# A two-layer network and a mixture-of-experts block: the two heads of a pair of attention heads taken half a step apart

## What is computed

```python
def mla_attention(q_nope, q_rope, k_nope, k_rope, v):      # 16 heads, 64 + 32 wide, values 64
    def block(args):                                        # one block of 128 queries
        s = (q_nope @ k_nope + q_rope @ k_rope) * scale
        s = where(chunk_mask(qpos, kpos), s, -inf)          # keys up to the query's chunk of 64
        return softmax(s) @ v
h = x + (mla_attention(...) * silu(gate)) @ w_o

def windowed_gqa(q, k, v, rel_bias, sink):                  # 8 heads of 64, 2 heads of keys
    def one_block(i):                                       # 128 queries, the keys of 3 blocks
        logits = where(valid, q @ k * scale + bias, -inf)
        m = maximum(max(logits), sink)
        p = exp(logits - m);  denom = sum(p) + exp(sink - m)
        return (p / denom) @ v
```

## Time and profile before

| | us |
|---|---|
| median of three timed runs | 3162.92 (3157.32 to 3166.98) |
| the profiled execution, its own time | 3188.76 |
| its span | 3187.0 |
| layer 1's attention, first scores to last output (1456.4 to 1879.5) | 423 |
| local attention, first scores to last output (2169.0 to 2361.6) | 193 |
| TensorE busy over the span | 2664.9 (84%) |
| VectorE busy | 1906.5 (60%) |
| ScalarE busy | 1089.6 (34%) |
| GpSimd busy | 577.8 (18%) |

### The profile page before, as it was taken

How to read it: one execution, slowest core, us unless ns; L and a number is a source line. 1 busy time by engine, 2 the same in 40 slices (tenths; PEclk the granted TensorE clock), 3 DMA queues, 4 the chain that set the end, 5 groups by cost and what they waited for, 6 DMA issues and landing times. The chain is left out here.

```text
span 3187.0 us, 31052 instructions
## 1 busy us (share of the span) xinstructions
PE 2664.9 (84%) x11101; PEld 1639.1 (51%) x11101; DVE 1906.5 (60%) x3678; ACT 1089.6 (34%) x1737; POOL 577.8 (18%) x503
## 2 busy tenths in 40 slices
PE   7699989689898898796899979966982498988887
PEld 4244434456666453344556645553532376766666
DVE  2099999665554200144777644054747787887786
ACT  2011110234433211433334323034423265655554
POOL 0000000111100000004677740000120022222211
PEclk9799999799999899898999999977995699999999
DMA  6500010210000221214343324002114498998896
GB/s 122 86 31 27 7 66 37 103 40 27 21 34 7 94 73 33 58 60 156 113 119 102 103 76 142 3 27 100 46 50 176 178 339 317 346 339 296 320 332 203
DMA packets 128007, 383.10 MB, mean 120 GB/s; under 512 B 27640, under 2 KB 34632, under 8 KB 126320
## 3 DMA queue, kind: packets, MB, share of 16 engines
q1 hardware_dynamic: 109104, 317.13, 27.7%
q0 software_dynamic: 18752, 64.00, 8.5%
HBM read 331.79 MB, written 49.31 MB: 120 GB/s over the span
## 5 line engine op out<-in xcount | busy, mean ns | idle before, releaser
L437 PE MATMUL ps<-l_hT,l_w 128*128 128x512 f32 x832 | 367.8, 602 | 26.6 <-DMA l_w<-in_e_w_in 26.6
L437 PEld LDWEIGHTS ps<-l_hT,l_w 128*128 128x128 f32 x832 | 159.2, 193 | 231.2 <-issue 202.4
L441 PE MATMUL ps<-l_w,l_hT 128*128 128x512 f32 (+3 forms) x768 | 256.9, 494 | 0.0
L441 PEld LDWEIGHTS ps<-l_w,l_hT 128*128 128x128 f32 x768 | 137.2, 193 | 115.2 <-issue 92.8
L1063 ACT ACTIVATE a_p<-ps,a_stat 128x384 f32<-128x384 f32 (+7 forms) x192 | 129.1, 672 | 189.9 <-DVE a_stat L1104 189.8
L2458 POOL DMA_INDIRECT out_dram<-x_y,e_token x16 | 101.6, 6353 | 506.1 <-DVE x_y L2583 506.1
L1367 DVE MAX8 l_best<-sel 128x8 f32<-128x384 f32 (+5 forms) x192 | 171.5, 893 | 5.4
L1368 DVE MATCH_REPLACE8 sel<-l_best,sel 128x384 f32<-128x384 f32 (+5 forms) x192 | 168.1, 875 | 0.0
L964 PE MATMUL ps<-l_kT,l_qTb 96*128 96x512 f32 (+3 forms) x384 | 145.4, 502 | 14.8 <-DMA l_qTb<-qT_d 14.8
L979 PE MATMUL ps<-ident,a_p 128*128 128x128 f32 x752 | 121.2, 290 | 36.7 <-DVE a_p L1122 35.3
L2312 DVE TENSOR_TENSOR x_w1l<-x_raw,x_w1h 128x4096 fp32r<-128x4096 f32 x32 | 141.5, 4422 | 17.0 <-ACT x_w1h L2304 17.0
(11 more groups left out here) (321 smaller groups left out, 5227.5 us busy)
## 6 DMA issues: line engine op xcount, KB each, us to landing
x_raw<-in_w_gate SPq DMA_DIRECT2D x32, 2048.0 KB, 13.2
x_raw<-in_w_up SPq DMA_DIRECT2D x32, 2048.0 KB, 13.3
x_raw<-in_w_down SPq DMA_DIRECT2D x32, 2048.0 KB, 8.2
ada_w<-in_w_ada POOLq DMA_DIRECT2D x64, 384.0 KB, 3.7
l_w<-in_e_w_in SPq DMA_DIRECT2D x7, 2048.0 KB, 8.2
x_d<-a_y SPq DMA_DIRECT2D x16, 512.0 KB, 2.6
qT_d<-l_qT SPq DMA_DIRECT2D x8, 768.0 KB, 4.3
l_qTb<-qT_d SPq DMA_DIRECT2D x8, 768.0 KB, 8.9
```

Of the source, the lines that this page charges most:

```text
L437: last = nc.tensor.matmul(self.t.ps[:, bank, :], w[:, c, col * P:(col + 1) * P], hT[:, c, half * 512:(half + 1) * 512], start=c == 0, stop ...
L441: last = nc.tensor.matmul(self.t.ps[:, bank, 0:s.n], hT[:, c, j * P:(j + 1) * P], w[:, c, 0:s.n], start=c == 0, stop=c == self.kc - 1)
```

## The change

It alters the order of the work in `PairAttention`, and who copies. A step now covers three pairs: the current one, the next, and the one after that (`far`). Side 0 of a pair runs half a step ahead of side 1. TensorE does: transposes of group 0, scores (next, 1), transposes of group 1, the piece of the projection, scores (far, 0), the sum. In the local attention scores (next, 1) and (far, 0) stand together ahead of the projection. VectorE does: its copies if it has any, normalisation (next, 0), maximum (next, 1), maximum (far, 0), normalisation (next, 1), output. ScalarE does: exponential (next, 0), all its copies, exponential (next, 1). In layer 1 ScalarE copies both sides; in the local attention the caller keeps side 1 on VectorE. The narrow pairs' score banks are numbered by side first, the semaphore of the scores is split by side, and the load of the queries waits for side 1's. The diff also has branches for joined pairs, for a bias in two parts and a hook `pe_aside_turn`; neither caller uses them, and they are left out here.

```diff
@@ -898,7 +899,7 @@
-        mover = mover or (lambda side: "act" if side == 0 else "dve")
+        mover = mover or (lambda side: "act")
...
-        self.scored, self.topped, self.exped = sem(f"{tag}_scored"), sem(f"{tag}_topped"), sem(f"{tag}_exped")
+        self.scored_by = k.sems(f"{tag}_scored", 2)
+        self.topped, self.exped = sem(f"{tag}_topped"), sem(f"{tag}_exped")
...
@@ -933,13 +935,14 @@
     def S(self, u, side):
         if self.pairs[u].width > 512:
             return self.t.ps[:, 2 * side:2 * side + 2, :].rearrange("p b n -> p (b n)")
-        return self.t.ps[:, 2 * (u % 2) + side, :]
+        return self.t.ps[:, 2 * side + u % 2, :]
 
     def steps(self):
 
         U = len(self.pairs)
-        for s in range(-1, U):
-            yield s + 1 if s + 1 < U else None, s if s >= 0 else None
+        some = lambda u: u if 0 <= u < U else None
+        for s in range(-2, U):
+            yield some(s + 2), some(s + 1), some(s)
...
-    def pe_scores(self, e, u, side=None):
-        nc, pair = self.k.nc, self.pairs[u]
-        if self.q_ready and side in (None, 0):
-            self.q_ready(e, u)
-        wide = pair.width > 512 or u and self.pairs[u - 1].width > 512
-        older = 2 * u if wide else 2 * (u - 1)
-        if older > 0 and side in (None, 0):
-            e.wait_ge(self.exped, older)
-        cuts = range(0, pair.width, 512)
-        for c, i in [(c, i) for c in cuts for i in ((0, 1) if side is None else (side,))]:
-            m, c1 = pair.maps[i], min(c + 512, pair.width)
-            last = nc.tensor.matmul(self.S(u, i)[:, c:c1], m.lhsT, m.rhs[:, c:c1], start=True, stop=True)
+    def pe_scores(self, e, *heads):
+
+        nc = self.k.nc
+        todo = []
+        for u, side in heads:
+            pair = self.pairs[u]
+            if self.q_ready and side == 0:
+                self.q_ready(e, u)
+            older = u - 1 if pair.width > 512 or u and self.pairs[u - 1].width > 512 else u - 2
+            if older >= 0:
+                e.wait_ge(self.exped, 2 * older + side + 1)
+            todo += [(c, side, u) for c in range(0, pair.width, 512)]
+        for c, side, u in sorted(todo):
+            pair = self.pairs[u]
+            m, c1 = pair.maps[side], min(c + 512, pair.width)
+            last = nc.tensor.matmul(self.S(u, side)[:, c:c1], m.lhsT, m.rhs[:, c:c1], start=True, stop=True)
             if c1 == pair.width:
-                last.then_inc(self.scored, 1)
+                last.then_inc(self.scored_by[side], 1)
...
     def pe(self, e):
-        for nxt, cur in self.steps():
-            pieces, groups = self.pieces(cur) if cur is not None else [], len(self.pairs[cur].groups) if cur is not None else 0
-            if self.tiled and nxt is not None:
-                self.pe_scores(e, nxt)
-            for g in range(2):
-                if g < groups:
-                    self.pe_turn(e, cur, g)
-                if self.tiled:
-                    self.pe_pieces(e, pieces[g * len(pieces) // 2:(g + 1) * len(pieces) // 2])
-                elif nxt is not None:
-                    self.pe_scores(e, nxt, g)
+        for far, nxt, cur in self.steps():
+            groups = len(self.pairs[cur].groups) if cur is not None else 0
+            first = [(far, 0)] if far is not None else []
+            second = [(nxt, 1)] if nxt is not None else []
+            if groups:
+                self.pe_turn(e, cur, 0)
+            self.pe_scores(e, *(second + first if self.tiled else second))
+            if groups > 1:
+                self.pe_turn(e, cur, 1)
+            if cur is not None:
+                self.pe_aside_turn(e, cur)
+                self.pe_pieces(e, self.pieces(cur))
             if not self.tiled:
-                self.pe_pieces(e, pieces)
+                self.pe_scores(e, *first)
             if cur is not None:
                 self.pe_sum(e, cur)
         self.pe_pieces(e, self.last_pieces())
+
+    def pe_aside_turn(self, e, u):
+        pass
 
...
     def act(self, e):
-        for nxt, cur in self.steps():
-            groups = len(self.pairs[cur].groups) if cur is not None else 0
-            if groups:
-                self.move(e, "act", cur, 0)
+        for _, nxt, cur in self.steps():
             if nxt is not None:
                 self.act_exp(e, nxt, 0)
-            if groups > 1:
-                self.move(e, "act", cur, 1)
+            if cur is not None:
+                for g in range(len(self.pairs[cur].groups)):
+                    self.move(e, "act", cur, g)
             if nxt is not None:
                 self.act_exp(e, nxt, 1)
             if cur is not None:
...
-        e.wait_ge(self.scored, v + 1)
-        S, top = self.S(u, side), st[:, 0, s]
+        e.wait_ge(self.scored_by[side], u + 1)
+        S, top, far = self.S(u, side), st[:, 0, s], None
...
         if m.adds[0][1] is None:
             c = m.adds[0][0]
             link(nc.vector.memset(S[0:CHUNK, c:c + CHUNK], NEG))
             link(nc.vector.reduce_max(top, S[:, 0:m.width], AX.X))
-            nc.vector.tensor_scalar(st[:, 1, s], top, -self.scale, None, ALU.mult).then_inc(self.topped, 1)
-        else:
...
+        if far is not None:
+            nc.vector.tensor_scalar(st[:, 1, s], top, far, -self.scale, ALU.max, ALU.mult).then_inc(self.topped, 1)
+        elif m.sink is not None:
             link(nc.vector.tensor_scalar(top, top, self.scale, m.sink, ALU.mult, ALU.max))
             nc.vector.tensor_scalar(st[:, 1, s], top, -1.0, None, ALU.mult).then_inc(self.topped, 1)
+        else:
+            nc.vector.tensor_scalar(st[:, 1, s], top, -self.scale, None, ALU.mult).then_inc(self.topped, 1)
...
     def dve(self, e):
         self.link.eng = e
-        for nxt, cur in self.steps():
-            groups = len(self.pairs[cur].groups) if cur is not None else 0
-            if self.tiled:
-                if nxt is not None:
-                    self.dve_top(e, nxt, 0)
-                    self.dve_top(e, nxt, 1)
-                for g in range(groups):
+        for far, nxt, cur in self.steps():
+            if cur is not None:
+                for g in range(len(self.pairs[cur].groups)):
                     self.move(e, "dve", cur, g)
-            else:
-                for g in range(2):
-                    if g < groups:
-                        self.move(e, "dve", cur, g)
-                    if nxt is not None:
-                        self.dve_top(e, nxt, g)
             if nxt is not None:
                 self.dve_norm(e, nxt, 0)
+                self.dve_top(e, nxt, 1)
+            if far is not None:
+                self.dve_top(e, far, 0)
+            if nxt is not None:
                 self.dve_norm(e, nxt, 1)
             if cur is not None:
                 self.dve_out(e, cur)
...
             def load_q(n):
                 if n >= 2:
-                    e.wait_ge(at.scored, C_HEADS * (n - 1))
+                    e.wait_ge(at.scored_by[1], at.per * (n - 1))
                 e.dma_start(qT[n % 2][:].rearrange("p h n -> p (h n)"), t.qT_d[order[n]]).then_inc(q_in[n % 2], 16)
...
         at = PairAttention(k, "a2", t, pairs, W_DIM ** -0.5, True,
                            lambda n, b, c: yfT[:, c, b * P:(b + 1) * P] if c < 4 else at.mixT[n % 2][:, c - 4, :], wo,
-                           (w_in, 32), None, add_end)
+                           (w_in, 32), None, add_end, mover=lambda side: "dve" if side else "act")
```

More of the change, by code:

```diff
@@ L996, in pe_sum, with chunk_ready @@
                     pT = self.pT[self.turns[u, g, side].slot][:, j * P:(j + 1) * P]
-                    r = slice(64 * side, 64 * side + 64)
-                    last = nc.tensor.matmul(self.t.ps[r, 6, 0:P], pair.values(c + j, side), pT, start=first, stop=stop)
+                    if pair.joined:
+                        last = nc.tensor.matmul(self.t.ps[:, 6, 0:P], pT, pair.values(c + j, side), start=first, stop=stop)
+                    else:
+                        r = slice(64 * side, 64 * side + 64)
+                        last = nc.tensor.matmul(self.t.ps[r, 6, 0:P], pair.values(c + j, side), pT, start=first, stop=stop)
             last.then_inc(self.summed, 1)
+    def chunk_ready(self, e, n, c):
+        e.wait_ge(self.mixed, self.per * n + max(0, c - (KD - self.per)) + 1)
     def pe_pieces(self, e, pieces):
@@ L1097, in dve_top, with add_max @@
         m, s = pair.maps[side], slice(v % 8, v % 8 + 1)
-        e.wait_ge(self.scored, v + 1)
-        S, top = self.S(u, side), st[:, 0, s]
+        e.wait_ge(self.scored_by[side], u + 1)
+        S, top, far = self.S(u, side), st[:, 0, s], None
+        def add_max(c, tile):
+            part = S[:, c:c + tile.shape[1]]
+            return nc.vector.tensor_tensor_reduce(out=part, in0=part, in1=tile, scale=1.0, scalar=-3.0e38,
+                                                  op0=ALU.add, op1=ALU.max, accum_out=top)
         if m.adds[0][1] is None:
@@ L1115, in dve_norm @@
         v = 2 * u + side
-        s = slice(v % 8, v % 8 + 1)
```

(17 more changed lines are left out.)

14 lines of the change are left out of this document (10 added, 4 removed).

## The result

| | before | changed |
|---|---|---|
| median of the timed runs, same chip | 3160.12 (3156.22 to 3166.98, 4 runs) | 3193.12 (3185.15 to 3198.09, 4 runs) |
| ratio, 95% interval | | 1.0085 (1.0066 to 1.0103) |
| profiled execution, its span | 3188.76, 3187.0 | 3185.15, 3183.4 |
| layer 1: first scores to last weighted sum | 422.7 | 426.4 |
| local attention: first scores to first transposes of the last pair | 187.9 | 207.1 |

The changed kernel is **slower by 0.85%**, 21 to 33 us, where no change was forecast; 3193 lies outside the range of 3142 to 3182. The two profiled spans hide this. The router and the experts, which the diff doesn't touch and which take about a quarter of the span, took 826 us in one profiled execution and 806 in the other, and 795 to 835 in those of the experiments. So the stages are compared, from one marked instruction to another.

What follows compares the result with a forecast made beforehand. TensorE was taken as the bound, with little idle outside k = 8. Terms +16 (k = 1 to 6), -3 (k = 7), -13 (k = 8) and 0 (local attention) sum to 0; plus a microsecond for a clock dip, 3164 us, range 3142 to 3182.

Steps and rivals of the forecast that it cites:

- the paragraph on the local attention: Local attention: copies keep their engines, TensorE is busy throughout, so the long stretch stays at 156.15 us; priced at 0.
- the part ahead of the stretch: Local attention's four steps without output projection: later start costs what a shorter step saves, 0, between -2 and +2 us.
- The fourth rival: Chain 0.2 us longer from a hold-up in normalise (next, 0) or output copy; 60 steps, +11, 3174 us; chance 0.12.
- The chain D: Layer 1, time from far scores through maximum to normalisation (next, 1) and transposes: 1.59 us at k = 1, 2.56 at k = 6.
- the cover C: Layer 1, TensorE's sum plus side-0 transposes, behind which the chain runs: 0.47 us at k = 1, 1.90 at k = 6.
- the 40 of the sum: Layer 1, k = 1 to 6: waits by which chain exceeds cover, 5.0 us summed, times 8, 40 us.
- The gate's 1.6 us: Layer 1, k = 1 to 6: what is left of 6.0 us of waits for a gate loaded late.
- F: Layer 1, TensorE's floor for a step without a wait: 7.23 us at k = 6, 0.86 less per key tile fewer.
- The evictions: Layer 1: 96 copies of transposed probabilities move from VectorE to ScalarE, beside other work everywhere; priced at nothing.
- The third: Rival for layer 1: TensorE's clock falls at k = 1 to 3, +12, 3176 us; chance 0.15.
- The first: Rival: the normalisation that counts seldom meets GpSimd's work, -15, 3149 us; chance 0.20.
- The second: Rival: waits vanish and TensorE runs at its floor; about -19, -5 and -17 in three stretches, 3123 us; chance 0.06.

Runs made afterwards that it cites:

- e5: Changed kernel with layer 1's scores (far, 0) made ahead of the projection's piece instead of behind it; 3165.24 us, one run (before 3163.01).
- e6: Changed kernel with layer 1's VectorE doing normalisation (next, 1) ahead of maximum (far, 0); 3179.86 us, one run (before 3163.01).
- e9: Changed kernel with the old class's local attention and layer 1's scores (far, 0) ahead of the projection's piece; 3159.65 us against 3186.05 before, ratio 0.991.
- e7: Changed kernel with layer 1's copies of side 1 back on VectorE; 3233.73 us, one run (before 3163.01).
- e4: Changed kernel with the local attention's scores ahead of the transposes, as before, stagger kept; 3177.53 us, one run.
- e10: Changed kernel with local scores ahead of the transposes and GpSimd's two instructions there cut to 8 columns; 3170.3 us, one run (before 3186 on that chip).
- e2: Kernel before with only the local attention written by the new class; 3180.34 us, ratio 1.0067 to before.
- e8: Kernel before with all of layer 1's copies on ScalarE and no stagger; 3162.41 us, one run (before 3163.01).

## Why the prediction was wrong

**The failed step** is the paragraph on the local attention: "with TensorE busy throughout, the stretch of 156.15 us stays", priced at 0. It takes 174.58. Measured against before's profile the local attention costs 19.3 us: 8.7 (GpSimd), 5.9 (TensorE's order) and 4.7 at the start, of which 3.3 are the average over the runs. What was given for the part ahead of the stretch, 0 between -2 and +2, held (+0.8); the start's loss is in the step after them. The forecast took a busy TensorE as proof that the stage can't change. It made two assumptions that no row supported:

- *that the matmuls' durations are independent of their order.* A busy engine at its floor can get a higher floor. The new order put the scores between transposes and projection, which use the same part of the array; such a pair of neighbours was not in the trace of before, so it needed a bound.
- *that the normalisations meet the same work of GpSimd as before.* The forecast weighed this hold-up for layer 1, and looked only there. In the local attention GpSimd's work starts at a fixed point, behind ScalarE's second half of the output, and the stagger moved the normalisation to that point and two maxima behind it. The fourth rival (a hold-up in normalise (next, 0) that also pushes the maximum) had the right mechanism in the wrong stage, and its price for layer 1 (+11) has nothing to do with the 8.7 found.

For the first, a price stood in the trace of before. Ahead of the modulation's matmuls, which use the same part of the array, a projection piece of layer 1 takes 1.72 us, start to start; ahead of the sum, `128*64`, it takes 1.81:

```profile
1560.47 1.88 PE L1011 MATMUL ps<-l_wo,a_mixT 128*128 128x512 f32 x4
1562.19 0.73 PE L1823 MATMUL ps<-ada_ones,ada_acc 128*128 128x1 f32 x6
```

With 0.09 us on either side of the scores, 27 steps make 5 us.

**k = 1 to 6: +16 forecast, +18.0 measured.** The chain D against the cover C holds: e5 and e6 break it in two ways and get 20 to 24 us back. Its size holds as well. Over the 48 steps the transposes of group 0 take 33.2 us more, start to start, than they do without a wait (0.27, 0.49, 0.71 and 0.93 us for 1 to 4 key tiles), and the eleven modulation sums stand for another 7.2: 40.4 against the 40 of the sum. That the total came within 2 us is in part luck. The gate's 1.6 us does not appear, and a projection piece ahead of scores takes 1.72 us instead of the 1.81 in F (4 us less); against these stands a stretch at half clock from 1555.8 to 1559.2, in which the step takes 7.59 us, and smaller terms.

**k = 7: -3 forecast, -5.7 measured.** Right in direction, but for another reason. The wait for GpSimd's modulation sums, for which 1.3 us were left, does not appear. In before it was 2.4 us, and the clock was 0.50 from its end on, 1825.6 to 1832.4, so that this one step took 13.85 us, in the changed kernel 9.33; the six others took 51.5 and 50.1 together. The wait is back in e5 and e9, which reach k = 7 earlier.

**k = 8: -13 forecast, -8.5 measured.** In the forecast 57.2 us pass between the first side-1 transposes and k = 1; in the trace it is 61.3 (1461.72 to 1523.02). The first of these steps ran at a granted clock of 0.75: two scores that take 1.88 us at full clock took 3.62, and the step 10.4 instead of 7.74. The forecast allowed for half clock only up to these transposes. In e5, where the first step had full clock, k = 8 is 12.1 us shorter than before. The first side-1 transposes start where forecast: 1468.7 forecast, 1469.0 measured, once the 7.3 us by which the stage begins earlier are added. The evictions, priced at nothing, were part of this gain and not beside it: with side 1's copies left on VectorE the gain is gone (e7, one run).

**Together** layer 1 gave +3.7 against 0. Add 19.3 and it is 23 us, inside the 21 to 33 of the timed runs, against 1 forecast.

**The rivals.** The third (clock at k = 1 to 3) did not come: 0.99 from k = 1 to 6, with one stretch at half clock. The first (the normalisation seldom meets GpSimd) neither: one of 128 columns takes 0.495 us in the mean, against 0.543 before. The second (no waits) did not come either; even e9, with e5's order, has 260.7 us there, 27 below the changed kernel and 10 above what that rival gives.

## What to carry to other kernels

A stage in which TensorE is always busy can still become slower, by a new order of TensorE's own work and by what moved work of the other engines now meets. For the first, count how often neighbouring matmuls change between 64 and 128 rows or columns of the array (96 rows beside 128 cost nothing here), and read the price of a change from pairs that the trace has. For the second, when normalisations move in time, look up in each stage what GpSimd does at that moment and what is queued behind them. And a stagger pays only if the cover goes with it: late scores behind the projection undid in layer 1 what the same stagger gives with them ahead of it.

## What the hardware showed beyond the forecast

- A VectorE normalisation of 384 columns took 2.39 us beside a GpSimd addition of 1024 columns (2.34 us), 0.42 alone; an addition of one column took 1.03 and 1.47 us instead of 0.15. The maxima and copies of 384 columns that read PSUM beside the same two instructions kept their 0.55 to 0.57 (before, changed).
- Scores on 64 rows of the array between transposes and projection on all of it cost about 0.2 us a step (6.09 against 5.89), and this shows as longer matmuls, not as idle time. A change between all of the array and 64 of its columns costs 0.09 us (1.81 against 1.72).
- The granted clock was 0.50 (1.2 GHz) in the local attention's first four steps of the changed kernel, against 0.58 before. In step 4 a projection piece of eight instructions, 3.60 us at full clock, took 4.68, and the step 9.78 us. In all six kernels with the new order that step takes 9.7 to 10.3 us, in the four of the old class 5.9 to 7.6, in e4 and e10 6.8 and 7.5.
- TensorE's wait of 2.4 to 2.5 us for GpSimd at k = 7 is in five kernels (before, e2, e5, e8, e9), and in each of them the clock falls to 0.50 within 2 us of its end; in before from 1825.6 to 1832.4, while TensorE is busy for 6.66 of the 6.80 us. In the seven others, with 1.1 us (e6) or no such wait, it stays at 1.00 there.
